# Down weights of experts 61 and 62 begun by GpSimd in two pieces of 9 and 119 rows

## The chip, the cores and the metric

The kernel runs on one core of one Trainium2 chip. Its time is the device time of one execution in microseconds (us); smaller is better. Every execution is one launch that computes the whole output from the inputs in the chip's memory.

## What is computed

The program is two transformer blocks over 512 tokens of width 1024, all in fp32. The part that matters here is the last stage of the second block, a mixture of 64 small experts: each token goes to two of them, and each expert is three matrices of 1 MB.

```
def expert_block(args):
    xb, e = args
    hid = jax.nn.silu(xb @ w1[e]) * (xb @ w3[e])     # gate and up: 1024 x 256 each
    return hid @ w2[e]                               # down: 256 x 1024
ys = lax.map(expert_block, (xs, block_e)).reshape(n_slots, dm)
ys = ys * slot_gate[:, None]
out = jnp.zeros((n_tok + 1, dm)).at[slot_tok].add(ys)[:n_tok]
```

A final norm follows, and the sum is stored. The weights of the experts are 64 x 3 MB, two thirds of all that the program reads.

## The kernel before

The program is written by hand for each engine, with semaphores between them. The first block, then the attention of the second, fill the first 920 us or so. Then the experts run one after the other, b = 0 to 63, in 16 bunches of four.

**Loading.** SyncE (SP) begins all weight transfers of the experts, in one order: `gate_up_in(e + 1)`, which is two transfers of 1 MB (w1 and w3, L734), then `down_in(e)`, one transfer of 1 MB (w2, L740). Each is 128 rows of 8 KB, one for each partition of SBUF. Gate and up weights have six places, down weights five. So before it begins `down_in(e)` SP waits until `s_my` is at least e - 4, that is, until TensorE has done the down product of expert e - 5, whose place is taken over. `gate_up_in(e + 1)` waits in the same manner on `s_gu`. The last seven transfers in SP's order are w1, w3 of 62; w2 of 61; w1, w3 of 63; w2 of 62; w2 of 63. In the program's names a place is a part of a larger tile: the places of gate and up weights of experts 60 and 61 lie in `big`, those of 62 and 63 in `wring`, that of 59 in `hT`; the down weights of 60 and 61 lie in `big`, those of 62 and 63 in `wring`.

**Computing.** For expert b TensorE (PE) runs `gate_up` (64 matmuls, L1769), which waits for both its weights, `s_e13`; then products that belong to the bunch before (L1822, L1823); then `expert_out(b - 1)`, the down product of the expert before (16 matmuls, L1797), which waits for `s_e2`; then `hidden_of(b)` (L1783). ScalarE and VectorE take the products out of PSUM. Ahead of `gate_up` of expert 63 stand six matmuls, `idle_turns(6)` (L1816), whose result isn't used. After it come `hidden_of(63)`, `expert_out(62)` and `expert_out(63)`, and then the last bunch is added up by token (L1961), normed and stored.

**GpSimd (POOL).** In this stage it begins one transfer, the row of the final norm's gains (`gainrow`, 128 rows of 4 KB, L2788), and then has nothing to do until the four powers of the final norm (`row_roots`, L2668), the first of which it waits for during 473 us.

Of the kernel before, what the change touches and what calls it, by code (L numbers as in the profile page):

```python
# [18 lines left out]
C = 32  # L19
E_SLOTS = 6  # L20
D_SLOTS = 5
BUNCH = 4


class Count:
# [9 lines left out]
    def wait(self):  # L35
        self.eng.wait_ge(self.sem, self.n)
# [12 lines left out]
def program(nc, x, meta_tokens, attn_norm, ffn_norm, final_norm, fox_w_in, fox_b_f, fox_q_norm, fox_k_norm,  # L49
            fox_w_out, ffn_w_in, ffn_w_out, attn_norm_2, ffn_norm_2, final_norm_2, gla_w_in, gla_w_gate,  # L50
            gla_b_gate, gla_out_norm, gla_w_o, moe_w_group, moe_w_expert, moe_w1, moe_w3, moe_w2, out):
    _, SEQ, D = x.shape
    META = meta_tokens.shape[0]
    T = SEQ // P
# [27 lines left out]
    with ExitStack() as ctx:  # L82
# [3 lines left out]
        def sem(name):  # L86
            return ctx.enter_context(nc.semaphore(name))
# [224 lines left out]
        s_rtw = sem("router_weights_in")  # L312
        s_e13 = [sem(f"expert_gate_up_in_{i}") for i in range(E_SLOTS)]
        s_e2 = [sem(f"expert_down_in_{i}") for i in range(D_SLOTS)]
        s_E = sem("choices_ready")
        s_gcP = sem("gate_column_done")
        s_gc = sem("gate_column_out")
# [20 lines left out]
        s_my = sem("moe_y")  # L338
# [18 lines left out]
        def add_tile(name, cols, parts, release=None, ends=None, hold=None):  # L357


            w = len(tiles)  # L360
            slot = w % W_SLOTS
            k = max(a + n for a, n, _, _ in parts)
            view = wring[:, slot * 4096:slot * 4096 + k * cols].rearrange("p (k n) -> p k n", k=k)
            slot_count[slot] += 16 * len(parts)
            if release is None:
                chunk_at[name] = len(chunks)
                for c in range(k if cols == 512 else 1):
                    chunks.append((name, c) if cols == 512 else (name, None))
                    if ends is None or c < k - 1 and cols == 512:
                        n_ck[0] += 1  # L370
                        released.append((s_ck, n_ck[0]))
                    else:
                        released.append(ends)
                release = hold or (s_lo, len(chunks))
            tile_names.append(name)
            tiles.append((slot, [(view[:, a:a + n, c:c + s.shape[2]], s) for a, n, c, s in parts], release))
            tile_at[name], tile_ready[name], tile_release[name] = view, (s_w[slot], slot_count[slot]), release
# [37 lines left out]
        for f0, f1 in halves:  # L415
# [3 lines left out]
            for j in range(2):  # L419
                n_out += 4  # L420
                out_tiles[f0, j] = []
                for a in range(f0, f1, 8):
                    n = min(8, f1 - a)
# [6 lines left out]
        for name, c0, n in (("a", 2 * QK + D, 1), ("q", 0, 1), ("k", QK, 1), ("v", 2 * QK, 2), ("r", 2 * QK + D + RANK, 2)):  # L430
            for j in range(n):
# [6 lines left out]
                parts = [(0, KD, 0, WG[:, :, c0 + j * 512:c0 + j * 512 + cols])]  # L438
# [152 lines left out]
        def w2_slot(i):  # L591
            return at2[i].rearrange("p (k n) -> p k n", k=KF)
# [3 lines left out]
        WW2 = moe_w2[0].rearrange("e (p k) n -> e p (k n)", k=KF)  # L596

        BUNCHES = EXPERTS // BUNCH
        R = BUNCH * C
        assert R == P and EXPERTS % BUNCH == 0  # L600
        HG, YG = P // 2, D // 4
# [77 lines left out]
        def _(sp):  # L679
# [48 lines left out]
            def gate_up_in(e, j, last=None):  # L728

                w13 = w13_slot(j)  # L730
                if last is not None:
                    sp.wait_ge(s_gu, last)
                for g, src in enumerate((W1, W3)):
                    sp.dma_start(w13[:, g, :, :].rearrange("p k n -> p (k n)"), src[e]).then_inc(s_e13[j], 16)  # L734

            def down_in(e, j, last=None):

                if last is not None:
                    sp.wait_ge(s_my, last)
                sp.dma_start(w2_slot(j).rearrange("p k n -> p (k n)"), WW2[e]).then_inc(s_e2[j], 16)  # L740
# [17 lines left out]
            down_in(4, 4)  # L758
            for e in range(D_SLOTS, EXPERTS):
                if e + 1 < EXPERTS:  # L760
                    gate_up_in(e + 1, (e + 1) % E_SLOTS, e + 2 - E_SLOTS)
                down_in(e, e % D_SLOTS, e + 1 - D_SLOTS)
            sp.wait_ge(s_tabs, 1)
            n_over = sp.value_load(ovf_i[0:1, SPILL:SPILL + 1], min_val=0, max_val=SPILL)
            with sp.If(n_over > 0):
                with sp.Fori(0, n_over) as i:
                    sp.wait_ge(s_my, i + EXPERTS)
                    e = sp.value_load(ovf_i[0:1, bass.ds(i, 1)], min_val=0, max_val=EXPERTS - 1)
# [15 lines left out]
        def _(act):  # L784
# [321 lines left out]
            def y_out(b, j, rows):  # L1106

                act.wait_ge(s_my, b + 1)
                for n in range(2):
                    last = act.copy(rows[:, n * YG:(n + 1) * YG], bank(6 + j % 2)[n * C:(n + 1) * C, 0:YG])  # L1110
                last.then_inc(s_myA, 1)

            def y_rows(b):
                return Y[b % BUNCH * C:(b % BUNCH + 1) * C, :]

            def y_of(b):

                if b % BUNCH == 0:
                    wait(act, s_yl, b // BUNCH)
                y_out(b, b, y_rows(b))  # L1120
# [83 lines left out]
        def _(pe):  # L1204
# [248 lines left out]
            for s in range(NS):  # L1453
                p, i = divmod(s, T)
# [16 lines left out]
            def output_sums(group, items, banks_ready, begun=0, together=False):  # L1471

                n = len(items)
                body = items[:n - CK_SLOTS] if together else items
                for i, (name, k, x, ready) in enumerate(body):
                    if i < begun:
                        continue
                    w = chunk(name, k)
                    if i == 0:
                        banks_ready()  # L1480
                    for t in range(T):
                        if t == 0 or i == 0:
                            ready(t)
                        last = three(bank(4 * group + t), cut(x, t * P, (t + 1) * P), w, i == 0, i == n - 1)
                        if i == n - 1:
                            last.then_inc(s_mO, 1)
                    if i < n - 1:
                        last.then_inc(s_ck, 1)
                if together:
                    rest, ws = items[len(body):], []  # L1490
                    for t in range(T):
                        for i, (name, k, _, ready) in enumerate(rest):
                            if t == 0:
                                ws.append(chunk(name, k))
                                ready(t)
                            w = ws[i]
                            last = three(bank(4 * group + t), cut(items[len(body) + i][2], t * P, (t + 1) * P), w,
                                         False, i == CK_SLOTS - 1)
                        last.then_inc(s_mO, 1)
# [292 lines left out]
            def down(j, slot):  # L1792

                w2 = w2_slot(slot)
                for k in range(KF):
                    for n in range(4):
                        last = pe.matmul(bank(6 + j % 2)[n * C:(n + 1) * C, 0:YG], mhT[j % 2][:, k * C:(k + 1) * C], w2[:, k, n * YG:(n + 1) * YG],  # L1797
                                         start=(k == 0), stop=(k == KF - 1), skip_group_check=True)
                last.then_inc(s_my, 1)

            def expert_out(b):

                pe.wait_ge(s_mhTe, b + 1)
                pe.wait_ge(s_e2[b % D_SLOTS], 16 * (b // D_SLOTS + 1))
                wait(pe, s_myA, b - 1)
                wait(pe, s_myD, b - 1)
                if b == 1:
                    pe.wait_ge(s_xT, 2)
                if b == 0:
                    pe.wait_ge(s_S4, 1)  # L1810
                down(b, b % D_SLOTS)

# [114 lines left out]
            with pe.If(n_over > 0):  # L1927
                with pe.Fori(0, n_over) as i:
# [15 lines left out]
                    pe.wait_ge(s_mhTe, i + (EXPERTS + 1))  # L1944
                    pe.wait_ge(s_e2[0], i * 16 + 16 * (EXPERTS // D_SLOTS + 2))
                    pe.wait_ge(s_myA, i + EXPERTS)
# [11 lines left out]
            for i in range(8):  # L1958
                t, n = divmod(i, 2)
# [675 lines left out]
        def _(pool):  # L2635
# [34 lines left out]
            def row_roots():  # L2670
                for t in range(T):
                    root(rstd[:, t:t + 1])
# [113 lines left out]
            row_roots()  # L2786
            pool.wait_ge(s_hnrow, T)
            pool.dma_start(gainrow[:, :], final_norm_2.rearrange("(a n) -> a n", a=1).to_broadcast([P, D])).then_inc(s_row2, 16)  # L2788

            row_roots()  # L2790

# [24 lines left out]
```

## Time and profile before

| | us |
|---|---|
| median of 3 runs | 1454.14 |
| lowest and highest | 1452.13, 1454.15 |
| span of the profiled execution, first to last instruction | 1449.5 |
| busy: TensorE matmuls | 1386.8 |
| busy: VectorE, ScalarE, GpSimd | 526.3, 522.3, 474.6 |

For the profiled execution the profile gives the span; the median of the runs is 4.6 us longer, which is what lies around it. TensorE is busy for 96% of the span. Of the 16 DMA engines that all transfers share, the mean busy share is 0.9 or more from about the 29th of 40 slices of the span on; this is the experts' stage. The profile doesn't tell the 16 apart: it gives their mean, and what all of them moved.

### The profile page before, as it was taken

To read this page: it belongs to the slowest core of one execution; us is meant where nothing else is said; L and a number is where in the kernel's file an instruction comes from. 1 tells how busy PE (TensorE), PEld (TensorE's weight loads), DVE (VectorE), ACT (ScalarE), POOL (GpSimd) and SP (SyncE) were. 2 spreads that over 40 slices of the span, in tenths; PEclk is the share of its full clock that TensorE was granted. 3 is DMA by queue.
4 is the path that set the end of the run, shared out by engine and by line. 5 is a ranking of instruction groups with operands and counts; after the bars stand their busy time and mean duration, and the time that the engine had idled before them with its cause. 6 is when DMAs were issued, how large, how long until landed. Compare 5 with 4: busy or idle time off the path is not lost. (4 is left out here: it accounts for less than half of the span.)

```text
span 1449.5 us, 26659 instructions
## 1 busy us (share of the span) xinstructions
PE 1386.8 (96%) x11116; PEld 1038.9 (72%) x11116; DVE 526.3 (36%) x1256; ACT 522.3 (36%) x1096; POOL 474.6 (33%) x457
## 2 busy tenths in 40 slices
PE   6999999999999999999989999999999999889986
PEld 5788886668788888888868786866666665555553
DVE  3102107752221200221244604264554554454435
ACT  4325438863422322322345533342223222222222
POOL 5334545553544444444355854410000000000000
PEclk9999999999999999999999999999999999999999
DMA  5133215304133124231232311669999999999994
GB/s 188 59 118 116 96 59 173 112 16 160 58 117 105 41 94 153 73 116 61 89 116 73 106 69 59 241 253 382 410 419 419 419 419 420 419 420 420 420 420 183
DMA packets 89561, 293.22 MB, mean 202 GB/s; under 512 B 9308, under 2 KB 38144, under 8 KB 64864
## 3 DMA queue, kind: packets, MB, share of 16 engines
q1 hardware_dynamic: 89040, 290.35, 51.9%
q8 instruction: 90, 1.47, 0.4%
q0 software_dynamic: 288, 1.05, 0.2%
q14 instruction: 31, 0.25, 0.0%
q10 hardware_dynamic: 112, 0.09, 0.0%
HBM read 289.27 MB, written 2.13 MB: 201 GB/s over the span
## 5 line engine op out<-in xcount | busy, mean ns | idle before, releaser
L496 POOL TENSOR_TENSOR wring_halves<-wring,wring_halves 128x512 fp32r<-128x512 f32 x274 | 356.6, 1306 | 379.9 <-ACT wring_halves L491 378.2
L491 ACT CAST wring_halves<-wring 128x512 fp32r<-128x512 f32 x274 | 168.3, 621 | 433.2 <-PE ps L1223 412.2
L1221 PE MATMUL ps<-wring_halves,big_halves 128*128 128x512 f32 x612 | 241.6, 395 | 3.7 <-POOL wring_halves L496 2.6
L1221 PE MATMUL ps<-hT_halves,wring_halves 128*128 128x512 f32 x480 | 187.4, 390 | 2.4 <-DVE big_halves L1981 2.4
L1222 PE MATMUL ps<-big_halves,wring_halves 128*128 128x512 f32 x480 | 186.8, 389 | 0.0
L1223 PE MATMUL ps<-hT_halves,wring_halves 128*128 128x512 f32 x480 | 186.7, 389 | 0.0
L2668 POOL TENSOR_TENSOR rstd<-rstd,half 128x1 f32<-128x1 f32 (+1 forms) x21 | 13.6, 647 | 507.7 <-DVE rstd L2621 478.5
L1222 PE MATMUL ps<-wring_halves,hT_halves 128*128 128x512 f32 x436 | 170.7, 391 | 0.0
L1223 PE MATMUL ps<-wring_halves,hT_halves 128*128 128x512 f32 x436 | 170.6, 391 | 0.0
L1221 PEld LDWEIGHTS ps<-wring_halves,big_halves 128*128 128x128 f32 x612 | 115.4, 189 | 31.9 <-POOL wring_halves L496 5.7
L1742 PE MATMUL ps<-xn,fixed 128*128 128x512 f32 x256 | 119.2, 608 | 1.1 <-DVE fixed L2416 1.1
L1221 PEld LDWEIGHTS ps<-hT_halves,wring_halves 128*128 128x128 f32 x480 | 90.1, 188 | 22.5 <-POOL wring_halves L496 2.9
L1223 PEld LDWEIGHTS ps<-hT_halves,wring_halves 128*128 128x128 f32 x480 | 90.1, 188 | 18.9
L1222 PEld LDWEIGHTS ps<-big_halves,wring_halves 128*128 128x128 f32 x480 | 90.1, 188 | 18.8 <-issue 0.2
L2506 DVE COPY arena<-ps 32x256 f32<-32x256 f32 x128 | 54.3, 425 | 120.6 <-PE ps L1797 116.0
L1223 PEld LDWEIGHTS ps<-wring_halves,hT_halves 128*128 128x128 f32 x436 | 82.3, 189 | 17.6
L1222 PEld LDWEIGHTS ps<-wring_halves,hT_halves 128*128 128x128 f32 x436 | 82.5, 189 | 16.5
L2539 DVE TENSOR_TENSOR xres<-xres,ps 128x512 f32<-128x512 f32 x128 | 82.5, 683 | 22.1 <-PE ps L1823 18.0
L2160 DVE TENSOR_TENSOR arena<-arena,ps 128x512 f32<-128x512 f32 x22 | 15.0, 684 | 195.4 <-ACT arena L971 195.4
L1742 PEld LDWEIGHTS ps<-xn,fixed 128*128 128x128 f32 x256 | 46.3, 191 | 54.6 <-issue 52.3
L1769 PE MATMUL ps<-big,arena 128*32 128x128 f32 x2048 | 65.9, 279 | 8.8 <-DMA big<-in_moe_w_dram 8.2
L1110 ACT COPY arena<-ps 32x256 f32<-32x256 f32 x128 | 46.3, 361 | 64.2 <-PE ps L1797 63.5
(348 smaller groups left out, 1986.3 us busy)
## 6 DMA issues: line engine op xcount, KB each, us to landing
big<-in_moe_w_dram SPq DMA_DIRECT2D x90, 1024.0 KB, 24.7
wring<-in_moe_w_dram SPq DMA_DIRECT2D x70, 1024.0 KB, 25.2
wring<-in_ffn_w_in_dram SPq DMA_DIRECT2D x22, 1024.0 KB, 7.3
hT<-in_moe_w_dram SPq DMA_DIRECT2D x20, 1024.0 KB, 24.3
wring<-in_fox_w_in_dram SPq DMA_DIRECT2D x7, 2048.0 KB, 8.7
wring<-in_gla_w_in_dram SPq DMA_DIRECT2D x6, 2048.0 KB, 7.9
mkv<-in_moe_w_dram SPq DMA_DIRECT2D x12, 1024.0 KB, 26.1
wring<-in_ffn_w_out_dram SPq DMA_DIRECT2D x4, 2048.0 KB, 7.8
```

What stands on the lines that cost most here:

```text
L491: act.copy(hi, src).then_inc(s_hi, 1)
L496: pool.tensor_tensor(lo, src, hi, ALU.subtract).then_inc(s_lo, 1)
L1110: last = act.copy(rows[:, n * YG:(n + 1) * YG], bank(6 + j % 2)[n * C:(n + 1) * C, 0:YG])
L1221: pe.matmul(out, lhs[1], rhs[0], start=start, stop=False)
L1222: pe.matmul(out, lhs[0], rhs[1], start=False, stop=False)
L1223: return pe.matmul(out, lhs[0], rhs[0], start=False, stop=stop)
L1742: last = pe.matmul(bank(n), one_hots(g)[1][:, t, :], xn[:, t, n * 512:(n + 1) * 512], start=(t == 0), stop=(t == T - 1))
L1769: last = pe.matmul(o[i * C:(i + 1) * C, 0:2 * HG], xeT[:, k, r * C:(r + 1) * C], w[:, :, i // 2, :, i % 2], start=(k == 0), stop=(k == KD ...
L2160: dve.tensor_tensor(prod[f % 2], sg[f % 2], bank((2 * f + 1) % 8), ALU.mult).then_inc(s_hid, 1)
L2506: last = dve.tensor_copy(rows[:, n * YG:(n + 1) * YG], bank(6 + j % 2)[n * C:(n + 1) * C, 0:YG])
L2539: dve.tensor_tensor(d, d, bank(n), ALU.add).then_inc(done, 1)
L2668: rooted.inc(pool.tensor_tensor(v, v, half[0:v.shape[0], 0:v.shape[1]], ALU.pow))
```

## The change

SP no longer begins `down_in(61)` and `down_in(62)`. GpSimd begins them, after its transfer of `gainrow`, each as two transfers: rows 0 to 8, and rows 9 to 127. It waits on the same values of `s_my` as SP did: 57 for expert 61, 58 for expert 62. TensorE waits for these two experts on semaphores of their own, for the full count of both pieces. The places, the bytes and the products are the same.

```diff
+DOWN_PARTS = {61: ((0, 9), (9, 128)), 62: ((0, 9), (9, 128))}
...
+        s_e2p = {e: sem(f"down_rows_of_{e}_by_gpsimd") for e in DOWN_PARTS}
...
             for e in range(D_SLOTS, EXPERTS):
                 if e + 1 < EXPERTS:
                     gate_up_in(e + 1, (e + 1) % E_SLOTS, e + 2 - E_SLOTS)
-                down_in(e, e % D_SLOTS, e + 1 - D_SLOTS)
+                if e not in DOWN_PARTS:
+                    down_in(e, e % D_SLOTS, e + 1 - D_SLOTS)
...
-                pe.wait_ge(s_e2[b % D_SLOTS], 16 * (b // D_SLOTS + 1))
+                if b in DOWN_PARTS:
+                    pe.wait_ge(s_e2p[b], 16 * len(DOWN_PARTS[b]))
+                else:
+                    pe.wait_ge(s_e2[b % D_SLOTS], 16 * (b // D_SLOTS + 1))
...
+            for e, parts in DOWN_PARTS.items():
+                rows = w2_slot(e % D_SLOTS).rearrange("p k n -> p (k n)")
+                pool.wait_ge(s_my, e + 1 - D_SLOTS)
+                for a, b in parts:
+                    pool.dma_start(rows[a:b, :], WW2[e][a:b, :]).then_inc(s_e2p[e], 16)
```

SP's last weight transfers before, from w1 of expert 62 on (w1, w2 and w3 are the matrices of the reference):

```order
L734 DMA wring<-in_moe_w1_2_dram 128x2048
L734 DMA wring<-in_moe_w3_2_dram 128x2048
L740 DMA big<-in_moe_w2_2_dram 128x2048
L734 DMA wring<-in_moe_w1_2_dram 128x2048
L734 DMA wring<-in_moe_w3_2_dram 128x2048
L740 DMA wring<-in_moe_w2_2_dram 128x2048 x2
```

The same place of SP in the changed program (all lines are two or more further down there):

```order
L736 DMA wring<-in_moe_w1_2_dram 128x2048
L736 DMA wring<-in_moe_w3_2_dram 128x2048
L736 DMA wring<-in_moe_w1_2_dram 128x2048
L736 DMA wring<-in_moe_w3_2_dram 128x2048
L742 DMA wring<-in_moe_w2_2_dram 128x2048
```

Between the weights of 62 and those of 63 nothing stands now, and behind them only w2 of 63. GpSimd's last instructions before:

```order
L2668 TENSOR_TENSOR rstd<-rstd,half 128x1 x4
L2788 DMA gainrow<-in_final_norm_2_dram 128x1024
L2668 TENSOR_TENSOR rstd<-rstd,half 128x1 x4
```

And in the changed program:

```order
L2674 TENSOR_TENSOR rstd<-rstd,half 128x1 x4
L2794 DMA gainrow<-in_final_norm_2_dram 128x1024
L2799 DMA big<-in_moe_w2_2_dram 9x2048
L2799 DMA big<-in_moe_w2_2_dram 119x2048
L2799 DMA wring<-in_moe_w2_2_dram 9x2048
L2799 DMA wring<-in_moe_w2_2_dram 119x2048
L2674 TENSOR_TENSOR rstd<-rstd,half 128x1 x4
```

The four transfers stand between `gainrow` and the powers of the final norm.

## Rows read from the trace of the kernel before

**Rows 1.** The page: GB/s in 40 slices, queues, DMA issues (KB, us to landing).

```profile
GB/s 188 59 118 116 96 59 173 112 16 160 58 117 105 41 94 153 73 116 61 89 116 73 106 69 59 241 253 382 410 419 419 419 419 420 419 420 420 420 420 183
...
q1 hardware_dynamic: 89040, 290.35, 51.9%
q8 instruction: 90, 1.47, 0.4%
q0 software_dynamic: 288, 1.05, 0.2%
...
big<-in_moe_w_dram SPq DMA_DIRECT2D x90, 1024.0 KB, 24.7
```

**Rows 2.** Timeline of TensorE's products: start us, us, engine, line, operation [idle before <-releaser].

```profile
1384.80 0.61 PE L1797 MATMUL ps<-big,arena 128*32 128x256 f32 x8
...
1389.66 1.07 PE L1797 MATMUL ps<-wring,arena 128*32 128x256 f32 x16
...
1395.17 3.57 PE L1769 MATMUL ps<-hT,arena 128*32 128x128 f32 x64 [3.04 <-DMA hT<-in_moe_w_dram]
...
1403.09 2.03 PE L1769 MATMUL ps<-big,arena 128*32 128x128 f32 x64
...
1410.09 2.03 PE L1769 MATMUL ps<-big,arena 128*32 128x128 f32 x64 [0.52 <-DMA big<-in_moe_w_dram]
...
1417.55 2.02 PE L1769 MATMUL ps<-wring,arena 128*32 128x128 f32 x64 [1.91 <-DMA wring<-in_moe_w_dram]
...
1420.63 1.07 PE L1797 MATMUL ps<-big,arena 128*32 128x256 f32 x16
...
1423.03 1.64 PE L1816 MATMUL ps<-fixed_halves 128*128 128x512 f32 x6
...
1424.97 2.06 PE L1769 MATMUL ps<-wring,arena 128*32 128x128 f32 x64 [0.30 <-DMA wring<-in_moe_w_dram]
...
1427.89 1.07 PE L1797 MATMUL ps<-wring,arena 128*32 128x256 f32 x16
...
1429.93 1.07 PE L1797 MATMUL ps<-wring,arena 128*32 128x256 f32 x16 [0.98 <-issue]
```

**Rows 3.** Windows: us, busy of PE, PEld, DVE, ACT, POOL, PEclk, DMA share, GB/s.

```profile
1375.00:1400.00 25.00, 20.96 (x285) 13.10 (x283) 7.60 (x18) 6.33 (x14) 0.00 (x0) 0.93 1.01 421
...
1418.00:1419.00 1.00, 1.00 (x44) 1.00 (x40) 0.00 (x0) 0.00 (x0) 0.00 (x0) 1.00 1.00 418
1419.00:1420.00 1.00, 1.00 (x24) 0.75 (x15) 0.10 (x1) 0.22 (x1) 0.00 (x0) 1.00 0.77 311
...
1423.00:1424.00 1.00, 1.00 (x8) 0.84 (x5) 1.00 (x3) 0.60 (x1) 0.00 (x0) 1.00 0.51 213
...
1427.00:1428.00 1.00, 0.40 (x11) 0.31 (x12) 0.22 (x1) 0.22 (x1) 0.00 (x0) 1.00 0.23 98
...
1429.00:1430.00 1.00, 0.07 (x4) 0.10 (x8) 0.85 (x2) 0.72 (x2) 0.00 (x0) 1.00 0.04 16
```

**Rows 4.** SyncE's queue in the timeline: start us, us, line, what it begins.

```profile
1393.64 2.13 SPq L740 DMA_DIRECT2D big<-in_moe_w_dram  x1
1395.81 4.32 SPq L734 DMA_DIRECT2D wring<-in_moe_w_dram  x2
1400.17 4.30 SPq L740 DMA_DIRECT2D wring<-in_moe_w_dram  x2
```

**Rows 5.** Transfers begun from 955 to 975: queue's packets, MB; KB each, us to landing.

```profile
q0 software_dynamic: 144, 0.52, 7.6%
...
mkv<-in_moe_w_dram SPq DMA_DIRECT2D x1, 1024.0 KB, 16.9
gainrow<-in_final_norm_dram POOLq DMA_DIRECT2D x1, 512.0 KB, 8.6
```

**Rows 6.** GpSimd in the timeline, and SyncE's issue of that mkv transfer.

```profile
964.17 0.64 POOL L2788 DMA_DIRECT2D gainrow<-in_final_norm_dram  x1 [1.79 <-DVE xn L2323]
1437.71 0.56 POOL L2668 TENSOR_TENSOR rstd<-rstd,half 128x1 f32<-128x1 f32 x1 [472.90 <-DVE rstd L2621]
...
965.28 0.33 SPq L740 DMA_DIRECT2D mkv<-in_moe_w_dram  x1
```

## The prediction

> **What bounds the kernel now.** I read the page first, by slices. From the 29th of 40 slices on the core reads 410 to 420 GB/s without a gap [rows 1], and TensorE's L1769 is found waiting for weights in the timeline: 3.04 us, 0.52, 1.91 and 0.30 us ahead of the gate and up products of experts 59, 61, 62 and 63 [rows 2]. So in the experts' stage the bytes set the pace, and TensorE comes close behind. One transfer of 1 MB is 1.049 MB / 420 GB/s = 2.50 us of all 16 DMA engines, and an expert is 7.5 us.
>
> Then I read the end in windows of 1 us, because the change touches only the last two experts. The rate is 418 GB/s until 1419 and falls in steps: 311, then 213 at 1423, 98 at 1427, 16 at 1429 [rows 3]. One DMA engine of 16 moves 420 / 16 = 26 GB/s, so about seven are through shortly after 1419 (213 / 26 is eight or nine still running), four run at 1427 and less than one in the last window. The sixteen are not level: some are ten microseconds ahead of the slowest. A transfer counts as landed when its slowest part is in, so every wait of TensorE is for the late ones. Why they are late these rows don't show by themselves. The instruction queue's 90 packets of 16 KB [rows 1] are work that the weights don't spread evenly, and are my guess for it.
>
> The path at the end, from rows 2: gate and up of 62 start at 1417.55, on their landing. From there to 1423.03 + 1.64 = 1424.67 TensorE is busy with no wait that the rows show: 7.12 us. Gate and up of 63 start at 1424.97, 0.30 us later, on their landing. The down product of 62 starts 2.92 us behind that, at 1427.89, and takes 1.07, until 1428.96. The down product of 63 starts only at 1429.93, 0.97 us later, although nothing but its weights can be missing: the transfers end in just that window [rows 3]. What follows, from 1429.93 to the end of the span, is compute and a store, and the change doesn't touch it. So behind the landing of 62's gate and up weights the end has 0.30 + 0.97 = **1.27 us** of waits for bytes. That is all that can be saved without an earlier landing of those weights.
>
> **SyncE's side.** It loses two issues of 2.13 to 2.15 us each [rows 4]. They are hidden: SP's transfers land 24.7 us after their issue in the median [rows 1], so a queue of some nine transfers stands in front of the DMA engines, and a SP that is 4 us earlier only makes it longer. The weights of 63 are issued 2.1 us earlier, worth nothing. The down weights of 63 still wait for expert 58's down product, and with about 20 us in hand. Value: 0.
>
> **GpSimd's side.** Four issues of about 0.64 us, as for gainrow [rows 6], on an engine that is idle for 472.90 us ahead of its next use at 1437.71. Its waits open when the down products of experts 56 and 57 end, at 1384.80 + 0.61 = 1385.4 and 1389.66 + 1.07 = 1390.7 [rows 2]. Behind these waits stand only the powers for the final norm, needed from 1437.7. Value: 0. If the descriptors took ten times as long, it would still be 0: expert 61's down product is at 1420.63 and 62's at 1427.89, 30 us on.
>
> **What moves in the queue.** This is the term that counts. Before, the down weights of 61 stood behind gate and up of 62, and those of 62 behind gate and up of 63. GpSimd has a queue of its own. How the two queues share the DMA engines is seen once: gainrow, issued at 964.17, landed 8.6 us later, while a transfer that SP issued at 965.28 took 16.9 us [rows 5, 6]. It didn't wait for what SP had queued. So both down transfers, issued at 1385.4 and 1390.7, go beside SP's backlog of 25 us, and are through by about 1400, in front of gate and up of 60 to 63 instead of behind those of 62 and 63. The bytes are the same, the rate is the same, and what was in front is later by what has overtaken it.
>
> By how much it is later for the **late** DMA engines depends on how 9 and 119 rows are spread, and no row of this trace shows a transfer of such a number of rows. gainrow's 128 rows left 144 packets [rows 5], which is 128 and one for each of the 16 engines. The nearest row therefore says: evenly, some 8 rows for each engine. Then gate and up of 59 to 62 land 2 x 2.50 = **5.0 us** later each (upper bound for an even spread 18 rows instead of 16, 5.6 us). Bounds for any spread: if the late ones get the 9-row pieces alone, one row of 8 KB each, it is 2 x 0.31 = 0.6 us; if each 119-row piece goes wholly to seven late ones, 17 rows each, it is 34 x 0.31 = 10.6 us. I take 5.0, the value for the one spread of which there is a row.
>
> **The sum.** The products of 62 start at 1417.55 + 5.0 = 1422.55. TensorE's 7.12 us bring it to 1429.67. The weights of 63 land at 1424.97 + 5.0 - 2.5 = 1427.5 (only w2 of 62 came from behind them), which is earlier, so the 0.30 us of wait is gone and TensorE is the last. Down product of 62 at 1429.67 + 2.92 = 1432.59, down product of 63 at 1432.59 + 1.07 = 1433.66; its weights are in at about 1429.9 as before, all bytes being the same, so the 0.97 us of wait is gone too. Against 1429.93 that is **+3.7 us**, that is 5.0 - 1.27. The span becomes 1449.5 + 3.7 = 1453.2, and with the 4.6 us by which the median stands above the span: 1454.14 + 3.7 = **1457.9**. The rule in one line: the end moves by the delay of 62's gate and up weights less 1.27 us.
>
> **The rivals.**
>
> *Same time, the uneven spread that helps.* If the 119-row pieces go to the seven DMA engines that are ahead, and the late nine get one row of each transfer, then the late ones are 2 x 7 rows = 4.4 us shorter at the end (1429.9 to 1425.5), and the early seven 2 x 9 rows = 5.6 us longer (1419.3 to about 1424.9): the steps of rows 3 would be level. For it speaks that 9 and 7 are close to what rows 3 say of late and early engines. Even so the path gains almost nothing: 62's weights land 0.6 us later, so the end moves by 0.6 - 1.27 = -0.7 us: **1453.5**. The 4.4 us end in a wait that TensorE's own 7.12 us cover. The same result, within 0.2%, if GpSimd's transfers are served in turn after all: 1454.1.
>
> The Trainium skill bears on this, in "DMA: Bandwidth & Descriptors", section "Why a DMA increments its semaphore by 16 and not by 1": a transfer runs on the largest number up to 16 that divides its rows, so on nine engines for 9 rows and on seven for 119, in turn from where GpSimd's last uneven one stopped. That would be this rival or the next; the same section says that some of GpSimd's transfers are spread by a sixteenth rounded up, eight rows each, which would be my forecast, 1457.9. No run here shows either.
>
> *Much slower, the spread that hurts.* 17 rows of each transfer go to late engines. Then 62's weights are 10.6 us late and the end 10.6 - 1.27 = 9.3 us: **1463.4**. The same size results if rows that one engine writes for another's partitions slow both down. This decides from a delay of 1.27 + 2.9 = 4.2 us on to be measurable. Against it: at most nine, and no more, are late.
>
> The skill's page "SBUF — State Buffer", section "Door 1: The DMA port swizzle (why `[64,N]` ≈ `[32,N]`)", says that eight partitions share a port of about 27 GB/s, whichever engine writes. By that an engine can't take rows off a late neighbour for free, and the helpful spread would cost as much as the even one, 1457.9, or more. The trace doesn't show it.
>
> *Faster.* The late engines' 4.4 us at the end count in full, because TensorE's 7.12 us in front of 63 shrink when the weights are in (they hold six matmuls for nothing, 1.64 us) or because the weights of 62 come earlier too: 1454.1 - 4.4 = **1449.7**. Against it: L1816 is issued whatever has landed.
>
> **How the numbers follow.** A measurement of this kernel can tell about 0.2%, 2.9 us, from no change. Forecast, 5.0 us of delay: 0.38, its own range 1456.5 to 1459.5. Same time (uneven and helpful, or served in turn): 0.33. Much slower: 0.16. Faster: 0.13. So faster 0.13, same 0.33, slower 0.54. The range of 8 in 10 leaves out the faster case and what of the much slower one lies above its price: from 0.6 us below 1453.5 to just above 1463.4, 1452.9 to 1463.8.
>
> **What would show it.** Right: the products of 59 to 62 each start about 5 us later than before, at 1422.5 for the last; no wait at L1769 for 63; both down transfers landed before 1402; the rate after 1419 falls in the same late steps, to 1430. The helpful spread: 418 GB/s until about 1424, then a fall within 1 to 2 us, and the products of 62 at 1418.1. The hurtful one: long steps, with a wait ahead of 61 and 62 of several us. Wrong altogether: GpSimd's transfers landing after 1410 (then nothing overtakes), or a path between the products of 62 and 63 shorter than 7.1 us.

## The result, and the profile after

| | before | after |
|---|---|---|
| median of the runs, us | 1453.58 (6 runs) | 1463.18 (6 runs) |
| span of the profiled execution, us | 1449.5 | 1461.7 |

One run of before took 2740 us and is left out of the comparison; the other five have a median of 1453.02, 10.2 us below that of after. The measured ratio of after to before is 1.0077, 95% interval 1.0065 to 1.0090: **slower by 11.2 us (9.4 to 13.1)**. The forecast was slower, by 3.7 us. The direction held and the size didn't: a third of it was seen coming. The 1463.18 lies inside the stated range, 1452.9 to 1463.8, but at its upper end, which was there for a rival with a chance of 0.16.

The page of after has GpSimd's transfers on their queue, q0, with 3.15 MB in place of 1.05 [rows 1]. The total of bytes is unchanged, and GpSimd's queue has 640 packets for 288 (in these lines and all below the columns are those of the lines ahead of the prediction).

```profile
GB/s 186 68 107 115 96 93 157 92 69 104 89 85 115 71 103 115 105 68 87 62 115 109 79 116 26 271 289 397 420 419 419 420 418 421 419 420 419 417 317 126
...
q1 hardware_dynamic: 88752, 288.26, 51.5%
q0 software_dynamic: 640, 3.15, 0.8%
```

The same products of TensorE as in [rows 2], now L1772 (gate and up, 58 to 63 in turn) and L1800 (down):

```profile
1385.78 2.97 PE L1772 MATMUL ps<-big,arena 128*32 128x128 f32 x64 [1.88 <-DMA big<-in_moe_w_dram]
...
1404.98 3.64 PE L1772 MATMUL ps<-hT,arena 128*32 128x128 f32 x64 [11.71 <-DMA hT<-in_moe_w_dram]
...
1415.37 2.03 PE L1772 MATMUL ps<-big,arena 128*32 128x128 f32 x64 [1.49 <-DMA big<-in_moe_w_dram]
...
1422.81 2.06 PE L1772 MATMUL ps<-big,arena 128*32 128x128 f32 x64 [0.96 <-DMA big<-in_moe_w_dram]
...
1430.19 3.00 PE L1772 MATMUL ps<-wring,arena 128*32 128x128 f32 x64 [1.81 <-DMA wring<-in_moe_w_dram]
...
1438.80 2.04 PE L1772 MATMUL ps<-wring,arena 128*32 128x128 f32 x64
...
1441.69 1.93 PE L1800 MATMUL ps<-wring,arena 128*32 128x256 f32 x32
```

The products of 59 wait 11.71 us for their weights, where they waited 3.04. From there everything is late, and the last two down products run back to back (one line of 32 matmuls) with no wait between them. That last point is as forecast.

Single executions are shifted against each other by a few us before the change begins to act. So from here on I count from the products of expert 58, which start before GpSimd's first transfer has slowed anything (in after its pieces are issued from 1383.97 on, and the rate from 1383 to 1387 is still 426 GB/s): 1386.19 us in before, in this line,

```profile
1386.19 2.03 PE L1769 MATMUL ps<-big,arena 128*32 128x128 f32 x64 [0.51 <-DMA big<-in_moe_w_dram]
```

and 1385.78 in after. To the products of 62 it was 31.36 us and is 44.41: **13.05 us later**, not 5.0. To the end of the last down product it was 44.81 (1431.00) and is 57.84 (1443.62): +13.0 us, near the +12.2 of the span and at the upper end of what the runs show (+11.2, 9.4 to 13.1).

Where the eight other microseconds come from is seen in a window of 20 us, first of before, then of after:

```profile
1388.00:1408.00 20.00, 16.96 (x228) 11.64 (x221) 8.01 (x18) 4.11 (x11) 0.00 (x0) 0.91 1.01 420
```

```profile
1388.00:1408.00 20.00, 8.29 (x108) 5.92 (x104) 3.77 (x8) 1.53 (x4) 1.04 (x2) 0.67 1.02 237
1409.00:1426.00 17.00, 14.55 (x204) 10.14 (x206) 6.89 (x15) 4.21 (x9) 0.00 (x0) 0.96 1.00 413
```

The last column is GB/s, the one ahead of it the busy share of the 16 DMA engines. **They are as busy as before (1.02) and move little more than half (237 GB/s for 420).** After 1409 the rate is back. The missing bytes are 20 us x 183 GB/s = 3.7 MB, 8.7 us at the full rate. GpSimd's issues and landings lie in this window:

```profile
1383.97 1.08 POOL L2799 DMA_DIRECT2D big<-in_moe_w_dram  x2 [421.52 <-PE ps L1800]
1392.21 1.04 POOL L2799 DMA_DIRECT2D wring<-in_moe_w_dram  x2 [7.16 <-PE ps L1800]
...
big<-in_moe_w_dram POOLq DMA_DIRECT2D x1, 952.0 KB, 15.2
wring<-in_moe_w_dram POOLq DMA_DIRECT2D x1, 952.0 KB, 16.5
```

They land after 15.2 and 16.5 us, by 1409.2 at the latest, and that is where the low stretch ends. (In the kernel with whole transfers, below, they took 10.5 and 10.2 us.)

### The profile page after: what moved, and what is told of

It reads as the page before. It is cut to its first block and busy times, and to the rows that moved or that the text cites. A ratio compares the mean times of both kernels' runs of the same rounds, so it can differ in the third digit from the quotient of the medians.

```text
span 1461.7 us, 26661 instructions
## 1 busy us (share of the span) xinstructions
PE 1388.2 (95%) x11116; PEld 1040.8 (71%) x11116; DVE 526.5 (36%) x1256; ACT 522.1 (36%) x1096; POOL 477.6 (33%) x461
## 3 DMA queue, kind: packets, MB, share of 16 engines
q1 hardware_dynamic: 88752, 288.26, 51.5%
q0 software_dynamic: 640, 3.15, 0.8%
## 5 line engine op out<-in xcount | busy, mean ns | idle before, releaser
L1225 PEld LDWEIGHTS ps<-wring_halves,hT_halves 128*128 128x128 f32 x436 | 82.4, 189 | 16.5
L1772 PE MATMUL ps<-big,arena 128*32 128x128 f32 x2048 | 65.9, 279 | 11.8 <-DMA big<-in_moe_w_dram 11.5
L1107 ACT ACTIVATE arena<-ps 128x64 f32<-128x64 f32 x64 | 14.3, 223 | 161.8 <-PE ps L1772 161.6
```

Of the source, the lines that this page charges most:

```text
L1225: pe.matmul(out, lhs[0], rhs[1], start=False, stop=False)
L1772: last = pe.matmul(o[i * C:(i + 1) * C, 0:2 * HG], xeT[:, k, r * C:(r + 1) * C], w[:, :, i // 2, :, i % 2], start=(k == 0), stop=(k == KD ...
```

## Experiments

Nine kernels, one of which ("The transfers by themselves") has no time to compare and no row here. The verdicts are ratios to runs of before on the same chip, and several chips were used, so two kernels are compared by their distances to before; "us" is the ratio less one, times 1450. The delays of 62's products and of the last down product's end are counted from the products of 58, as above.

| kernel | ratio, 95% interval | us | GB/s while the pieces pass | products of 62, us later | end of last down product, us later |
|---|---|---|---|---|---|
| after | 1.0077, 1.0065 to 1.0090 | +11.2 | 237 | 13.1 | 13.0 |
| e1_whole | 1.0037, 1.0025 to 1.0050 | +5.4 | 419 | 4.9 | 4.7 |
| e2_halves | 1.0101, 1.0081 to 1.0120 | +14.6 | 275 | 11.4 | 11.4 |
| e3_sp_pieces | 1.0146, 1.0125 to 1.0166 | +21.2 | 241 | 5.7 | 17.7 |
| e4_only62 | 1.0039, 1.0025 to 1.0053 | +5.7 | 258 | 6.8 | 5.6 |
| e6_sp_halves | 1.0086, 1.0065 to 1.0108 | +12.5 | 294 | 5.9 | 10.6 |
| e7_only62_whole | 1.0006, 0.9994 to 1.0017 | +0.9 | | 2.4 | 1.2 |
| e8_turns | 1.0021, 1.0011 to 1.0031 | +3.0 | | 4.4 | 2.8 |
| e9_columns | 1.0016, 1.0003 to 1.0029 | +2.3 | 419 | 4.2 | 2.7 |

### GpSimd, but whole transfers

```diff
-DOWN_PARTS = {61: ((0, 9), (9, 128)), 62: ((0, 9), (9, 128))}
+DOWN_PARTS = {61: ((0, 128),), 62: ((0, 128),)}
```

> GpSimd begins the down weights of 61 and 62 as in the changed kernel, but each as one transfer of 128 rows. Measured for the changed kernel: 9.6 us over before, with the rate at about 240 GB/s in place of 420 from 1387 to 1408. Theory A (crossing): pieces of odd size are dealt to DMA engines that then write partitions which another DMA engine also writes, and both slow down; whole transfers don't. Then the rate stays at 420 GB/s, the products of 62 start 5.0 us later than before and the end moves by 5.0 - 1.27 = +3.7 us. Theory B (uneven): 119 rows go to seven engines, the others run dry: whole transfers are even, the same +3.7. Theory C (anything begun by GpSimd beside SyncE's backlog is slow, whatever its shape): the low stretch stays, +9 us or so.

Windows of 20 us and the products of 58, 62 and 63 with the last down products:

```profile
1388.00:1408.00 20.00, 13.97 (x194) 9.82 (x193) 7.33 (x15) 3.58 (x9) 0.53 (x1) 0.83 1.01 419
```

```profile
1385.41 2.03 PE L1772 MATMUL ps<-big,arena 128*32 128x128 f32 x64 [0.52 <-DMA big<-in_moe_w_dram]
...
1421.67 3.39 PE L1772 MATMUL ps<-wring,arena 128*32 128x128 f32 x64 [2.93 <-DMA wring<-in_moe_w_dram]
...
1430.10 2.04 PE L1772 MATMUL ps<-wring,arena 128*32 128x128 f32 x64
...
1432.99 1.93 PE L1800 MATMUL ps<-wring,arena 128*32 128x256 f32 x32
```

The rate is 419 GB/s over the same 20 us, so GpSimd as the one that begins them costs no bandwidth (theory C falls). The products of 62 come at 1421.67 - 1385.41 = 36.26 us, 4.90 later than before: the 5.0 of the forecast. That holds for 62, which the sum uses; the forecast's "59 to 62 each" doesn't, since 59's products are only 1.9 us later here and 61's 3.9. The sum is then short by one thing. From the products of 62 to those of 63 it takes 8.43 us, where I had 7.12, because the products of 62 themselves take 3.39 us in place of 2.02. The cause is below ("Whole, with the wait of 62 filled"). This leaves the extra loss of after, 11.2 against 5.4 us, to the 9 and 119 rows, and two theories: crossing (A), or seven engines that carry 17 rows each (B).

### GpSimd, two pieces of 64 rows

```diff
-DOWN_PARTS = {61: ((0, 9), (9, 128)), 62: ((0, 9), (9, 128))}
+DOWN_PARTS = {61: ((0, 64), (64, 128)), 62: ((0, 64), (64, 128))}
```

> The same with two pieces of 64 rows each. 64 divides by 16, so by every rule each of the 16 DMA engines gets 4 rows of each piece, and nothing is uneven. Theory A (crossing): rows 0 to 63 dealt to all sixteen land in partitions that belong to eight of them, so the rate falls as in the changed kernel, to 300 GB/s or less for 10 us or more, and the end is +8 us or more. Theory B (uneven): no low stretch, +3.7 us. Theory C: as the changed kernel, +9.

```profile
1388.00:1408.00 20.00, 8.55 (x112) 5.88 (x114) 5.06 (x10) 2.04 (x5) 1.02 (x2) 0.74 1.01 275
```

275 GB/s with all DMA engines busy, and +14.6 us. An even number of rows doesn't help; B can't be the cause here. What is left is that there are two pieces, or that each holds only some of the partitions; the last kernel of this section parts the two.

### SyncE, pieces of 9 and 119 rows in the old places

```diff
-                if e not in DOWN_PARTS:
-                    down_in(e, e % D_SLOTS, e + 1 - D_SLOTS)
+                if e in DOWN_PARTS:
+                    rows = w2_slot(e % D_SLOTS).rearrange("p k n -> p (k n)")
+                    sp.wait_ge(s_my, e + 1 - D_SLOTS)
+                    for a, b in DOWN_PARTS[e]:
+                        sp.dma_start(rows[a:b, :], WW2[e][a:b, :]).then_inc(s_e2p[e], 16)
+                else:
+                    down_in(e, e % D_SLOTS, e + 1 - D_SLOTS)
...
-            for e, parts in DOWN_PARTS.items():
-                rows = w2_slot(e % D_SLOTS).rearrange("p k n -> p (k n)")
-                pool.wait_ge(s_my, e + 1 - D_SLOTS)
-                for a, b in parts:
-                    pool.dma_start(rows[a:b, :], WW2[e][a:b, :]).then_inc(s_e2p[e], 16)
```

> SyncE begins both transfers in its old places, in pieces of 9 and 119 rows; GpSimd has no part. Nothing is overtaken. Theory A with rows dealt evenly: two stretches of low rate of some 5 to 10 us each, later than before, near 1410 to 1425, +5 us or so. Theory B (nine and seven engines): by the rows 2 x 9 = 18 rows (5.6 us) more on seven engines and 14 fewer (4.4 us) on the nine; if the seven are the late ones +5 us or more, if they are the early ones the end moves by -1 to 0 us. Theory C: no change, since GpSimd is out.

```profile
1402.00:1414.00 12.00, 8.83 (x113) 5.95 (x109) 4.25 (x8) 2.48 (x6) 0.00 (x0) 0.86 1.04 241
...
1425.00:1430.00 5.00, 1.89 (x17) 0.71 (x17) 0.67 (x2) 0.00 (x0) 0.00 (x0) 0.75 0.72 188
1430.00:1435.00 5.00, 4.98 (x21) 3.21 (x22) 2.36 (x5) 1.45 (x3) 0.00 (x0) 0.57 0.40 129
1435.00:1440.00 5.00, 2.33 (x68) 1.91 (x68) 0.45 (x2) 0.22 (x1) 0.00 (x0) 1.00 0.18 77
```

The worst of all, +21.2 us where I had expected some +5, with GpSimd out of it and nothing overtaken. The same 241 GB/s at a full busy share appear, later, when SP's queue comes to these pieces. Behind it there is a long tail that none of GpSimd's kernels has: for fifteen microseconds the busy share is 0.72, then 0.40, then 0.18. A few DMA engines have much more left than the others. That fits pieces that SyncE's queue deals to nine and to seven engines, and so does its count of packets, here and in the kernel of SyncE's two pieces of 64 rows below:

```profile
q1 hardware_dynamic: 89040, 290.35, 52.1%
```

```profile
q1 hardware_dynamic: 89072, 290.35, 52.1%
```

The first is the count of before, to the packet [rows 1]: 9 and 119 rows together leave as many as 128 rows. Those leave 144 in this queue (two such transfers fewer were 89040 - 88752 = 288 packets fewer in after), 128 and 16 more, which I read as one for each engine that takes part. Two pieces on nine and on seven engines would leave the same 16; two pieces on all sixteen would leave 16 more for each expert, and the second line has those 32. The profile doesn't name the engines, and no run of mine takes the crossing out of this kernel. How much of the 21 us belongs to it stays open.

### Only expert 62

```diff
-DOWN_PARTS = {61: ((0, 9), (9, 128)), 62: ((0, 9), (9, 128))}
+DOWN_PARTS = {62: ((0, 9), (9, 128))}
```

> Only the down weights of 62 are moved to GpSimd, in 9 and 119 rows. Theory A: one low stretch of about 10 us in place of two that together make 21, so 62's gate and up weights are later by half of what the changed kernel shows (12.7 us there, 6 us here) and the end by 6.3 - 1.27 = about +5 us. Theory B: the same half. If the loss were a fixed cost of GpSimd's first transfer, +9 us would stay.

```profile
1393.00:1404.00 11.00, 7.61 (x96) 5.49 (x84) 3.78 (x8) 2.12 (x5) 0.00 (x0) 0.84 1.02 258
```

One stretch of 11 us at 258 GB/s, the products of 62 6.8 us later (half of 13.05 is 6.5), +5.7 us in all. The loss goes with the number of transfers that are cut (one or two here); it is no fixed cost of a first one.

### The transfers by themselves

The kernel before, with this behind the last store:

```diff
+            pool.wait_ge(s_out, 16 * (T + 1))
+            for i, (a, c) in enumerate(((0, 128), (9, 128), (0, 9), (0, 64), (0, 8))):
+                pool.dma_start(big[a:c, 4096:6144], WW2[i][a:c, :]).then_inc(s_one[i], 16)
+                pool.wait_ge(s_one[i], 16)
+            pool.dma_start(big[0:64, 4096:6144], WW2[6][0:64, :]).then_inc(s_one[5], 16)
+            pool.dma_start(big[64:128, 4096:6144], WW2[6][64:128, :]).then_inc(s_one[5], 16)
+            pool.wait_ge(s_one[5], 32)
```

> The kernel before, and behind its last store six transfers by GpSimd with nothing else in flight, each waited for before the next: 128 rows; rows 9 to 127; rows 0 to 8; rows 0 to 63; rows 0 to 7; and last rows 0 to 63 and 64 to 127 begun together. They write a free place and change no output; the kernel is longer by their time, so its time says nothing. Crossing theory: 128 rows move at about 400 GB/s, rows 0 to 63 alone at half of that, since all 16 DMA engines write into partitions of eight, so half the bytes take as long as the whole; 119 rows, dealt in order, at 200 to 300 GB/s. Seven-engine theory: 119 rows at 7 x 26 = 183 GB/s for 5.3 us, but rows 0 to 63 at about 400 GB/s, through in half the time of 128.

Windows in the middle of four of them: 128 rows, rows 9 to 127, rows 0 to 63, and the two halves together.

```profile
1450.50:1452.50 2.00, 0.00 (x0) 0.00 (x0) 0.00 (x0) 0.00 (x0) 0.00 (x0) 0.50 0.97 410
1455.50:1458.50 3.00, 0.00 (x0) 0.00 (x0) 0.00 (x0) 0.00 (x0) 0.00 (x0) 0.50 0.97 243
1465.00:1466.50 1.50, 0.00 (x0) 0.00 (x0) 0.00 (x0) 0.00 (x0) 0.00 (x0) 0.50 0.99 279
1474.50:1477.00 2.50, 0.00 (x0) 0.00 (x0) 0.00 (x0) 0.00 (x0) 0.00 (x0) 0.50 1.12 246
```

This is the disputed cost with nothing beside it, in one execution. The whole transfer moves 410 GB/s. The 119 rows, 93% of the same bytes, move 243 with the same busy share of 0.97. Seven engines would have shown a share of 7/16 = 0.44, so **GpSimd's 119 rows run on all, or all but one, of the DMA engines**, and each is slow: by share and rate a row of 8 KB takes an engine 0.31 us in the whole transfer and 0.52 us in this one (an estimate, 0.97 x 16 x 8.19 KB over the rate). The packets agree: the 119 rows leave 144 on GpSimd's queue, nine for each of 16 engines, as the 128 rows do. Half the partitions give 279, and both halves together, all 128 partitions in two pieces, still only 246. From issue to landing the whole takes 5.0 us, the 119 rows 6.6, the single half 4.6 and each of the two halves 6.2; the pieces of 9 and of 8 rows take 3.0 each. So half the bytes take nearly as long as all, as the crossing theory had it, but its rate was too low: I had expected 200 GB/s for the half. Its window holds most of that short transfer, so the 279 is rough.

What no row shows is which DMA engine writes which partitions. The Trainium skill has it, in "DMA: Bandwidth & Descriptors", section "The descriptor swizzle", and "SBUF — State Buffer", section "Door 1: The DMA port swizzle (why `[64,N]` ≈ `[32,N]`)": in a transfer of 128 rows each engine writes just the eight partitions of one port, and a port carries about 27 GB/s. A piece that is dealt otherwise would send several engines to one port. That is the crossing of theory A, and the lowered rates at full busy share agree with it in kind. In size they don't quite: for half the partitions the Trainium skill's table in that last section gives 196 GB/s measured and about 218 at most, and here it was 279 in the middle of the transfer. So that ports are the reason stays an argument. Nor does any run part the writing side from the reading side: a piece cut by rows is also one unbroken part of the matrix in the chip's memory.

### SyncE, two pieces of 64 rows in the old places

As in the kernel of SyncE's pieces above, with

```diff
-DOWN_PARTS = {61: ((0, 9), (9, 128)), 62: ((0, 9), (9, 128))}
+DOWN_PARTS = {61: ((0, 64), (64, 128)), 62: ((0, 64), (64, 128))}
```

> SyncE begins both down transfers in their old places in its order, each in two pieces of 64 rows. GpSimd has no part, nothing is overtaken, and 64 rows are even over 16 DMA engines. Crossing theory: the DMA engines stay busy and the rate halves while these pieces pass, about 4 x 1.25 us of work that takes twice as long on the early engines first, then on the late ones: 62's weights 2 to 5 us later and the end +3 to +9 us. If only GpSimd's transfers, or only uneven ones, cost: the time of before, within 0.2%.

```profile
1407.00:1417.00 10.00, 6.61 (x100) 4.28 (x103) 3.14 (x6) 2.10 (x4) 0.00 (x0) 1.00 1.02 294
...
1424.93 3.64 PE L1777 MATMUL ps<-wring,arena 128*32 128x128 f32 x64 [5.59 <-DMA wring<-in_moe_w_dram]
```

+12.5 us with even pieces, no GpSimd and nothing overtaken, above the 3 to 9 us that I expected: 294 GB/s at a share of 1.02, and a wait of 5.59 us ahead of 62. So cutting a transfer by rows costs on either queue. If the crossing cost as much in the kernel of 9 and 119 rows, the uneven spread would account for the other 21.2 - 12.5 = 8.7 us there; no run shows that it does.

### Only expert 62, whole

```diff
-DOWN_PARTS = {61: ((0, 9), (9, 128)), 62: ((0, 9), (9, 128))}
+DOWN_PARTS = {62: ((0, 128),)}
```

> Only the down weights of 62 are moved to GpSimd, whole, 128 rows. One transfer in place of two overtakes 62's gate and up weights: they are 2.5 us later (one MB at 420 GB/s), and by the rule of the prediction the end moves by 2.5 - 1.27 = +1.2 us, with up to 1.3 us more if the longer wait lowers TensorE's granted clock as it did in the kernel with both transfers whole. So +1.2 to +2.5 us, under or at the 0.2% that can be told. If the loss were a matter of GpSimd's transfer as such, it would be nearer to the +5.4 us of both.

```profile
1385.01 2.03 PE L1772 MATMUL ps<-big,arena 128*32 128x128 f32 x64 [0.52 <-DMA big<-in_moe_w_dram]
...
1418.79 2.03 PE L1772 MATMUL ps<-wring,arena 128*32 128x128 f32 x64 [1.74 <-DMA wring<-in_moe_w_dram]
...
1429.11 1.93 PE L1800 MATMUL ps<-wring,arena 128*32 128x256 f32 x32
```

62's products at 33.78 us from 58's, 2.4 later (expected 2.5), the end at 46.03, 1.2 later (expected 1.2 by "the delay less 1.27"). The runs say +0.9 us, interval -0.9 to +2.5. The rule of the prediction holds where its premise does.

### Whole, with the wait of 62 filled

The kernel with whole transfers, and eight matmuls without use ahead of the gate and up product of 62:

```diff
                 if b == EXPERTS - 1:
                     idle_turns(6)
+                if b == EXPERTS - 2:
+                    idle_turns(8)
                 expert_in(b)
```

> Both down transfers whole by GpSimd as in e1_whole, and eight more matmuls without use ahead of the gate and up product of 62, to fill some 2.2 us of its wait of 2.93 us. In e1_whole the granted clock fell in that wait, and the product of 62 took 3.39 us in place of 2.02. If the clock is the third term of the loss, the stretch from the products of 62 to those of 63 returns from 8.4 to about 7.1 us and the kernel is 1.3 us faster than e1_whole (+4.1 us over before in place of +5.4). If not, the same time as e1_whole.

```profile
1415.01 2.12 PE L1822 MATMUL ps<-fixed_halves 128*128 128x512 f32 x8
1417.06 2.03 PE L1772 MATMUL ps<-wring,arena 128*32 128x128 f32 x64
...
1424.11 2.03 PE L1772 MATMUL ps<-wring,arena 128*32 128x128 f32 x64
```

The products of 62 take 2.03 us, and it is 7.05 us from them to those of 63: the 7.12 of the forecast. In the kernel without the eight matmuls the granted clock of the window around these products was 0.66, here it is 1.00:

```profile
1420.00:1425.00 5.00, 3.33 (x65) 2.82 (x65) 0.00 (x0) 0.00 (x0) 0.00 (x0) 0.66 0.56 236
```

TensorE had waited 2.93 us there. The time fell from +5.4 to +3.0 us, where I had expected +4.1, and the intervals (3.6 to 7.2, and 1.6 to 4.5) overlap. What the two traces show is the size of the term: with the clock up it is 1.38 us less between the products of 62 and 63. That the eight matmuls kept it up isn't shown, since the next kernel has it up without them.

### Two pieces cut by columns

```diff
-DOWN_PARTS = {61: ((0, 9), (9, 128)), 62: ((0, 9), (9, 128))}
+DOWN_PARTS = {61: ((0, 1024), (1024, 2048)), 62: ((0, 1024), (1024, 2048))}
...
-                    pool.dma_start(rows[a:b, :], WW2[e][a:b, :]).then_inc(s_e2p[e], 16)
+                    pool.dma_start(rows[:, a:b], WW2[e][:, a:b]).then_inc(s_e2p[e], 16)
```

> GpSimd begins the down weights of 61 and 62 in two pieces each, but cut by columns: 128 rows of 4 KB and 128 rows of 4 KB. Four transfers, even, and each over all 128 partitions. Crossing theory: nothing crosses, the rate stays at 420 GB/s, and the time is that of e1_whole: 62's weights 5 us later, +4 to +6 us. If two pieces in flight on GpSimd's queue, or the count of transfers, make the DMA engines slow, it is that of e2_halves, +10 us or more, with the rate near 250 GB/s.

```profile
1388.00:1408.00 20.00, 13.88 (x196) 10.04 (x196) 8.15 (x18) 3.89 (x10) 1.81 (x4) 0.91 1.02 419
...
1387.72 1.04 POOL L2799 DMA_DIRECT2D big<-in_moe_w_dram  x2 [421.69 <-PE ps L1800]
```

The same four issues, the same engine, the same bytes in each piece as in the halves by rows, and 419 GB/s for 275: +2.3 us for +14.6. The number of transfers is not it; the cut through the partitions is. The +2.3 us (0.4 to 4.2) are below the +4 to +6 that I expected, and overlap the whole transfers' +5.4 (3.6 to 7.2). In its trace TensorE's clock stayed up for the products of 62 (2.03 us, shown at the end), as in the kernel of the eight matmuls, whose time it has within the intervals.

No kernel beats the one before; the nearest, one whole transfer moved, can't be told from it. By the forecast's reading 1.27 us of waits behind the landing of 62's weights is all that such a change could return, and each whole MB that overtakes costs about 2.4 us.

## Why the prediction was wrong, point by point

- **SyncE's side and GpSimd's side, 0 each: right.** In the kernel with whole transfers SyncE's earlier issues changed nothing that shows: the busy share was 1.01, as before. In after GpSimd's issues took 0.52 to 0.54 us each, and TensorE waited for neither of its down products.
- **GpSimd's transfers overtake: right.** Both had landed by 1409, ahead of 62's and 63's weights, though not by the forecast's 1402. Alone this makes 62's products 4.9 us later (forecast 5.0), 2.4 for one transfer (forecast 2.5).
- **"The bytes are the same, the rate is the same": this is the step that failed.** The rate was 237 GB/s in place of 420 for 20 us, so the 0.31 us for a row of 8 KB, on which the 2 x 2.50 us and their bounds stand, held for whole transfers only. The delay was 13.05 us: 4.9 for overtaking, as in the kernel with whole transfers, and the remaining 8.2 for the lost rate (8.7 by the missing bytes). I had looked for a row on how a piece of 119 rows is *spread*, and took gainrow's even spread over 16 engines as the nearest. That was right as to the number of engines, on GpSimd's queue. But gainrow is 128 rows, and that a piece which is no full set of partitions moves at another *rate* has no row in the trace of before. There I had only the port rule of the Trainium skill, and left it outside the sum, as "1457.9, or more".
- **The end moves by the delay less 1.27 us: right, but for the clock.** In after 13.05 + 1.19 - 1.21 = 13.03. The 1.21 are the last down products, 4.82 us behind 63's start in place of 6.03. The 1.19 are the stretch from 62 to 63, 8.61 us in place of 7.42: its wait of 0.30 us is gone as forecast, but it is longer by 1.49 because TensorE ran at half its clock (a granted 0.50, the lower level of 1.2 GHz, from 1431 to 1434) just behind the wait of 1.81 us. I had carried 7.12 us over from a place where the clock was at 1.00 into one where it fell. A window of after (the third number from the end is the clock):

```profile
1431.00:1432.00 1.00, 1.00 (x28) 1.00 (x24) 0.00 (x0) 0.00 (x0) 0.00 (x0) 0.50 0.56 238
```

- **The rivals.** The measured 1463.2 is at the price of "much slower" (1463.4, chance 0.16). Its first mechanism, 17 rows on each of seven late engines, is refuted for GpSimd's queue by the transfers alone: a busy share of 0.97 leaves room for one idle engine at most, not for nine. Its second, rows that one engine writes for another's partitions slow both down, is the one that the runs bear out: a cut through the partitions lowers the rate and a cut by columns doesn't. Who writes what isn't shown. That the number fits too is in part luck: the 10.6 us of delay were worked out for the first mechanism and borrowed for the second, whose delay was 13.05, and the +9.3 us for the end were +13.0 in the trace and +11.2 in the runs. GpSimd's transfers served in turn, one part of "same time" (0.33), fall with the landings after 10.5 and 10.2 us, where SyncE's took about 28 to 33. The helpful spread, the other part, rested on the same nine and seven engines and falls with them: the steps of the rate in [rows 3] did not get level. In after they still fall from 393 GB/s in 1422 to 25 in 1436. "Faster" found nothing for it.
- **Why some DMA engines are ten microseconds late** was a guess, that the instruction fetches do it, and no run tested it.

## What to carry to other kernels

Don't cut a transfer by rows to shift load between DMA engines: the pieces here (9 and 119 rows, 64 and 64) kept them as busy, and while they passed all traffic together moved 56 to 70% of the full rate (237 to 294 of 420 GB/s), on either queue; a cut by columns kept the rate at 419. A transfer that GpSimd began on a queue of its own didn't wait its turn, it delayed what was in front of it in the other queue (2.4 us for 1 MB), so look there for the price, not in the transfer itself. And where a change makes TensorE wait, give the stretch behind the wait a second price, at the lower clock: here 1.4 us more on 7.1.

## What was not expected of the hardware

- 64 rows and 64 rows, begun together with nothing beside them, move at 246 GB/s, against 410 for the same MB in one transfer. Among other traffic they slow that down as well: 275 GB/s for both together.
- The same cut costs more in SyncE's queue (9 and 119 rows: +21.2 us) than in GpSimd's (+11.2), although nothing is overtaken there, with a tail in which the busy share is down to 0.18.
- How long TensorE has waited doesn't alone say whether its clock is down behind the wait. It was down behind 2.93 us (whole transfers) and 1.81 us (after), where the products of 62 took 3.39 and 3.00 us, and up behind 1.52 us in the kernel cut by columns, and behind 3.33 us, ahead of 61, in SyncE's halves:

```profile
1423.75 2.03 PE L1772 MATMUL ps<-wring,arena 128*32 128x128 f32 x64 [1.52 <-DMA wring<-in_moe_w_dram]
```

```profile
1413.64 2.04 PE L1777 MATMUL ps<-big,arena 128*32 128x128 f32 x64 [3.33 <-DMA big<-in_moe_w_dram]
```
